# The second layer's modulation: chunk sums on VectorE, ScalarE and GpSimd instead of TensorE matmuls over all chunks

## The reference, cut to what matters

```
m = jax.nn.silu(cond) @ ada_w[layer] + ada_b[layer]      # cond: c or c_ctx, 1024 values; ada_w[layer]: 1024 x 6144
sh1, sc1, g1, sh2, sc2, g2 = m reshaped to 6 x 1024
h = rmsnorm(x, norm_g[layer, 0]) * (1 + sc1) + sh1
x = x + g1 * mixer(h)                                    # layer 0: convolution and retention; layer 1: attention
h = rmsnorm(x, norm_g[layer, 1]) * (1 + sc2) + sh2
x = x + g2 * (square(relu(h @ mlp_w1[layer])) @ mlp_w2[layer])
```

## Time and profile before

| | |
|---|---|
| median of three runs | 1569.05 us (1568.49 to 1569.4) |
| profiled execution, its span from first to last instruction | 1567.7 us; no time of its own is given beside the runs' |
| TensorE busy | 1546.3 us, 99% |
| VectorE, ScalarE, GpSimd busy | 986.4 (63%), 625.8 (40%), 487.8 us (31%) |
| strips of both layers on TensorE (L783) | 43.2 us |
| granted TensorE clock, mean | 0.996 |

### The profile page before, as it was taken

One profiled execution on the slowest core, in us unless ns is written; L12 is line 12 of the kernel. 1 busy time (PEld: TensorE's weight loads), 2 busy tenths in 40 slices (PEclk: granted clock), 3 DMA queues, 4 the chain that ended last, 5 costly groups with the idle time before them and its releaser, 6 DMA issues.

```text
span 1567.7 us, 28790 instructions
## 1 busy us (share of the span) xinstructions
PE 1546.3 (99%) x11992; PEld 1512.9 (97%) x11992; DVE 986.4 (63%) x1831; ACT 625.8 (40%) x1152; POOL 487.8 (31%) x350
## 2 busy tenths in 40 slices
PE   8999999999999999999999999999999999999998
PEld 7999999999999999999999999999999999999998
DVE  5348677675774755565555888773675755556555
ACT  5323333344432344234235534662433334523443
POOL 0233313314222344143235253101333334324431
PEclk9999999999999999999999999999999999999999
DMA  9454333313243344344343121001222132223212
GB/s 327 158 188 142 122 116 114 102 55 110 80 159 111 122 131 138 109 135 148 101 155 134 35 81 61 28 2 54 81 81 59 63 108 68 84 66 108 68 54 82
DMA packets 133410, 162.23 MB, mean 103 GB/s; under 512 B 4640, under 2 KB 108064, under 8 KB 133280
## 3 DMA queue, kind: packets, MB, share of 16 engines
q1 hardware_dynamic: 132048, 159.34, 31.6%
...
## 4 chain that ended last, share of the span: by engine, by line
PE 90%; DVE 5%; ACT 2%; issue 1%; DMA 1%; SPq 0%; POOL 0%; DVEq 0%; ACTq 0%
PE ps L664 59%; PE ps L1083 19%; PE ps L783 3%; PE ps L1275 2%; PE ps L1223 1%; DVE ps L1906 1%; PE ps L920 1%; PE ps L953 1%; DVE hL L1917 1%; DMA pre_w<-in_ada_w 1%; PE ps L869 1%; DVE ps L1896 1%; PE ps L949 1%; DVE amx L2503 1%; ACT wH L1319 1%
## 5 line engine op out<-in xcount | busy, mean ns | idle before, releaser
L1831 POOL TENSOR_TENSOR wL<-raw,wH 128x512 fp32r<-128x512 f32 x212 | 314.7, 1509 | 708.5 <-ACT wH L1319 513.7
L664 PE MATMUL ps<-fH,wH 128*128 128x320 f32 x1024 | 318.8, 311 | 0.2 <-DVE fL L2289 0.2
L664 PE MATMUL ps<-fH,wL 128*128 128x320 f32 x1024 | 316.6, 309 | 0.0
L664 PE MATMUL ps<-fL,wH 128*128 128x320 f32 x1024 | 316.6, 309 | 0.0
L1867 DVE SCALAR_TENSOR_TENSOR xT<-ps,modT,xT 128x192 f32<-128x192 f32 (+1 forms) x456 | 183.3, 434 | 192.0 <-PE ps L664 190.1
L1831 POOL TENSOR_TENSOR wL<-raw_high,wH 128x512 fp32r<-128x512 f32 x124 | 164.2, 1349 | 338.5 <-ACT wH L1342 209.7
L664 PE MATMUL ps<-hH,wH 128*128 128x320 f32 x704 | 221.3, 314 | 1.9 <-DVE hL L1917 1.1
L664 PE MATMUL ps<-hH,wL 128*128 128x320 f32 x704 | 217.8, 309 | 0.0
L664 PE MATMUL ps<-hL,wH 128*128 128x320 f32 x704 | 217.7, 309 | 0.0
L664 PEld LDWEIGHTS ps<-fH,wH 128*128 128x128 f32 x1024 | 192.5, 188 | 3.4 <-DVE xT L1867 1.2
L664 PEld LDWEIGHTS ps<-fL,wH 128*128 128x128 f32 x1024 | 192.5, 188 | 0.1
...
## 6 DMA issues: line engine op xcount, KB each, us to landing
...
raw<-in_mlp_w SPq DMA_DIRECT2D x64, 512.0 KB, 3.8
raw_high<-in_mlp_w SPq DMA_DIRECT2D x64, 512.0 KB, 3.8
raw<-in_even_w_in SPq DMA_DIRECT2D x28, 512.0 KB, 5.9
pre_w<-in_ada_w SPq DMA_DIRECT2D x16, 512.0 KB, 9.1
raw<-in_odd_w_qkv SPq DMA_DIRECT2D x10, 512.0 KB, 3.5
raw<-in_even_w_out SPq DMA_DIRECT2D x8, 512.0 KB, 3.6
raw<-in_odd_w_o SPq DMA_DIRECT2D x6, 512.0 KB, 3.5
```

The costliest lines, as they stand in the source:

```text
L664: last = nc.tensor.matmul(ps[:, bank, 0:width], a_, b_, start=(k == 0 and p_ == 0), stop=(k == nk - 1 and p_ == 2))
L1831: last = nc.gpsimd.tensor_tensor(wL[:, at % 4, cs], raw(t)[:, j, cs], wH[:, at % 4, cs].bitcast(F32), ALU.subtract)
```

## The change

Layer 1's modulation is no longer contracted on TensorE over eight chunks of 128 rows. For each condition s (c and c_ctx) the sum over chunks k of siluc[k, s] x ada[k] is formed elementwise (128 rows x 512 columns), and TensorE only sums its 128 partitions.

- **Loads.** `load_late(i)`, i = 0 to 47, loads 256 rows x 512 columns (512 KB, two chunks) into one half of `ada`, alternately. It waits until GpSimd is done with part i-2.
- **VectorE, `sum0(i)`:** two instructions of 128x512, ada_sum0 = part x siluc + ada_sum0 for c (the first of a block only multiplies).
- **ScalarE, `scale1(i)`:** waits for `sum0(i)`, then scales both chunks in place by c_ctx's values.
- **GpSimd, `sum1(i)`:** waits for that and adds both chunks to ada_sum1 (one instruction for the first part of a block, two for the others).
- **TensorE, `strips_of_sums(b)`:** after four parts, 8 matmuls: stationary a column of ones, moving ada_sum0, then ada_sum1.
- **Places.** Six slots per cycle: `LATE_AT(c, slot)` = 6c - 3 + slot, for parts 0 to 39. Slots 0, 1, 2 lie in the w1 half of a cycle, slots 3, 4, 5 in w2 (VectorE: after updates 5, 8, 14). TensorE's strips stand at slot 0 (after T3), 2 (after w2's first block) and 4 (before w2's last two groups), wherever a block is complete there. Parts 40 to 47 lie in the output projection and the start of layer 1's MLP; strips 10 stand after group 5 of the projection.
- The turned modulation adaT has one buffer instead of two; coefficients(3) and the last modulations move from the end of layer 0's MLP to the projection and to layer 1's first cycle; raw_high moves to the end of SBUF.

The core of the diff:

```diff
+        one_row = vecT[:, 0, R_ROW:R_ROW + 64].rearrange("p (c r) -> p c r", c=2)
...
+        def ada_part(i):
+
+            return ada[:, 2 * (i % 2):2 * (i % 2) + 2, :]
...
+            def load_late(i):
+
+                if i is None:
+                    return
+                if i < 2:
+                    sp.wait_ge(ada_strips, M_MLP)
+                else:
+                    sp.wait_ge(sum1_done, SUM1_AT(i - 1))
+                m, row0 = i // 4, 256 * (i % 4)
+                sp.dma_start(ada_part(i), ada_w[1, row0:row0 + 256, 512 * m:512 * m + 512]
+                             .rearrange("(k p) n -> p k n", p=P)).then_inc(late_in[i % 2], 16)
...
+                w1(0, 1)
+                late(0, 4)
...
                     w2(c, 0, (0, 1))
                     w2(c, 1, (0,))
-                    if layer == 0 and c:
-                        load_ada(M_MLP + 3 * c + 1)
+                    if c:
+                        late(c, 1)
+                        late(c, 2)
                     w2(c, 1, (1,))
-                    if layer == 0 and c == 0:
-                        load_ada(M_MLP + 1)
-                    if layer == 0:
-                        load_ada(M_MLP + 3 * c + 2)
                     if c < CYCLES - 1:
-                        w1(c + 1)
+                        if c:
+                            late(c, 3)
+                        w1(c + 1, 0)
+                        w1(c + 1, 1, (0,))
+                        if c:
+                            late(c, 4)
+                        w1(c + 1, 1, (1,))
+                        late(c, 5)
+                        late(c + 1, 0)
...
+            load_late(LATE - LATE_WO)
+            load_late(LATE - LATE_WO + 1)
             load_tile(T_WO + 3, k8(odd_w_o[0], 768))
+            for i in range(LATE - LATE_WO + 2, LATE):
+                load_late(i)
...
+            def strips_of_sums(b):
+
+                pe.wait_ge(sum0_done, 8 * b + 8)
+                pe.wait_ge(sum1_done, SUM1_AT(4 * b + 4))
+                pe.wait_ge(ada_turn, MOD_LAYER0 + b)
+                pe.wait_ge(vec_in, 16)
+                for c, total in enumerate((ada_sum0, ada_sum1)):
+                    by_lane = total[:].rearrange("p (b j r) -> p j b r", j=4, r=32)
+                    for j in range(4):
+                        last = nc.tensor.matmul(ps[32 * j:32 * j + 32, B_ADA, 0:P], one_row[:, c], by_lane[:, j],
+                                                start=(c == 0), stop=(c == 1), tile_position=(0, 32 * j))
+                last.then_inc(late_strips, 1)
...
-                part(0)
...
                     one(T3, S3, 0, m)
-                part(1)
+                strips_after(c, 0)
...
+                def strips_after(c, slot):
+
+                    i = LATE_AT(c, slot)
+                    if layer == 0 and i is not None and i % 4 == 3:
+                        strips_of_sums(i // 4)
...
-                        if layer == 0:
-                            hooks = {5: [lambda: strips(M_MLP)], 7: [lambda: strips(M_MLP + 1)]}
+                        if layer == 1:
+                            hooks = {5: [lambda: strips_of_sums(11)]}
...
-                        if q == 1:
-                            part(c)(2)
+                            if q == 3 and j == 1:
+                                strips_after(c, 4)
+                        if q == 0:
+                            strips_after(c, 2)
...
-                       (lambda half, k: pe.wait_ge(attn_ready, max(VALUES_OF["tiles", k], VALUES_OF["context", k // GRP]) + 1)) if t == 0 else None)
+                       (lambda half, k: pe.wait_ge(attn_ready, max(VALUES_OF["tiles", k], VALUES_OF["context", k // GRP]) + 1)) if t == 0 else None,
+                       {1: [lambda: strips_of_sums(10)]} if t else None)
...
+            def scale1(i):
+
+                if i is None:
+                    return
+                act.wait_ge(sum0_done, 2 * i + 2)
+                for k in range(2):
+                    last = nc.scalar.activation(ada_part(i)[:, k, :], ada_part(i)[:, k, :], ACT.Copy,
+                                                scale=siluc[:, 2 * (i % 4) + k, 1:2])
+                last.then_inc(scaled1, 1)
...
                         split_product(s, T1, t, g + 2)
+                        late(c, 0)
                         split_product(s, T4, t, g + 4)
                         hidden_pair(c, 0)
                         split_product(s, B22, t, g + 6)
                         split(t + 2, g + 8, (0,))
+                        late(c, 1)
                         hidden_pair(c, 2)
                         split(t + 2, g + 10, (1,))
                         hidden_pair(c, 4)
                         split(t + 3, g + 12, (0,))
+                        late(c, 2)
                         hidden_pair(c, 6)
                         split(t + 3, g + 14, (1,))
...
+                        if q != 2:
+                            late(c, (3, 4, None, 5)[q])
...
+                    if n < 2:
+                        scale1(40 + n)
                     square(3, n, V_WO, "tile")
+                    if n in (4, 5, 7):
+                        scale1({4: 42, 5: 43, 7: 44}[n])
                 split(T_WO + t + 2, G_WO + 4 * (t + 1))
             for n in range(8, 12):
                 square(3, n, V_WO, "tile")
+                if n > 8:
+                    scale1(45 + n - 9)
...
+            def sum1(i):
+
+                if i is None:
+                    return
+                pool.wait_ge(scaled1, i + 1)
+                a, b = (ada_part(i)[:, k, :] for k in range(2))
+                if i % 4 == 0:
+                    if i:
+                        pool.wait_ge(late_strips, i // 4)
+                    nc.gpsimd.tensor_tensor(ada_sum1[:], a, b, ALU.add).then_inc(sum1_done, 1)
+                else:
+                    for k, part in enumerate((a, b)):
+                        pool.wait_ge(sum1_done, SUM1_AT(i) + k)
+                        nc.gpsimd.tensor_tensor(ada_sum1[:], ada_sum1[:], part, ALU.add).then_inc(sum1_done, 1)
...
+            for c in range(1, CYCLES):
+                SUMS_AFTER[T_MLP0 + 4 * c + 2, 0] = (LATE_AT(c, 1),)
+                SUMS_AFTER[T_MLP0 + 4 * c + 3, 0] = (LATE_AT(c, 2),)
+                if c < CYCLES - 1:
+                    SUMS_AFTER["p", c + 1 - PLAIN, B11] = (LATE_AT(c, 3), LATE_AT(c, 4))
+                    SUMS_AFTER["p", c + 1 - PLAIN, B21] = (LATE_AT(c, 5), LATE_AT(c + 1, 0))
...
-                dve.wait_ge(ada_strips, 2 * block + 2)
-                nc.vector.transpose(adaT[:, block % 2, :], ps[:, B_ADA, 0:P]).then_inc(ada_turn, 1)
+                if block < MOD_LAYER0:
+                    dve.wait_ge(ada_strips, 2 * block + 2)
+                else:
+                    dve.wait_ge(late_strips, block - MOD_LAYER0 + 1)
+                if block:
+                    dve.wait_ge(mod_done, block)
+                else:
+                    dve.wait_ge(pre_mod, 4)
+                nc.vector.transpose(adaT[:], ps[:, B_ADA, 0:P]).then_inc(ada_turn, 1)
                 dve.wait_ge(ada_turn, block + 1)
                 m0 = N_PRE + 4 * block
-                nc.vector.tensor_tensor(modT[:, m0:m0 + 4, :], adaT[:, block % 2, :].rearrange("p (b c) -> p b c", c=32)[:, :, 0:2],
+                nc.vector.tensor_tensor(modT[:, m0:m0 + 4, :], adaT[:].rearrange("p (b c) -> p b c", c=32)[:, :, 0:2],
                                         vecT[:, 1, m0:m0 + 4, None].to_broadcast([P, 4, 2]), ALU.add).then_inc(mod_done, 1)
...
+            def sum0(i):
+
+                if i is None:
+                    return
+                dve.wait_ge(late_in[i % 2], 16 * (i // 2 + 1))
+                if i % 4 == 0 and i:
+                    dve.wait_ge(late_strips, i // 4)
+                for k in range(2):
+                    by, part = siluc[:, 2 * (i % 4) + k, 0:1], ada_part(i)[:, k, :]
+                    if i % 4 == 0 and k == 0:
+                        nc.vector.tensor_scalar(ada_sum0[:], part, by, None, ALU.mult).then_inc(sum0_done, 1)
+                    else:
+                        dve.wait_ge(sum0_done, 2 * i + k)
+                        nc.vector.scalar_tensor_tensor(out=ada_sum0[:], in0=part, scalar=by, in1=ada_sum0[:],
+                                                       op0=ALU.mult, op1=ALU.add).then_inc(sum0_done, 1)
...
+                    if n in (1, 2):
+                        sum0(46 + n - 1)
...
+                def late(c, slot):
+
+                    before = 6 * c - 3 + slot
+                    if layer == 0 and 0 < before <= LATE - LATE_WO and before % 4 == 0:
+                        modulation(MOD_LAYER0 + before // 4 - 1)
+                    if layer == 0:
+                        sum0(LATE_AT(c, slot))
...
-                    modulate(c, 0)
+                    late(c, 0)
                     t_lo(s, T4)
                     for m in range(2):
...
-                    modulate(c, 1)
+                    late(c, 1)
...
```

(13 more changed lines are left out.)

85 lines of the change are left out of this document (47 added, 38 removed).

## The result

The changed kernel takes **1625.99 us** (median of 4 runs, 1625.68 to 1626.18), the kernel before 1569.22 (4 runs). The ratio is 1.0362, with a 95% interval from 1.0347 to 1.0377. Slower, as forecast, but by 56.8 us instead of 29, and outside the range.

The account below looks back on a forecast made before the run. TensorE was taken as the bound: 19.6 us saved there, against waits of 30, 8.2, 8.3 and 2.3 us, made +29.2 on a median of 1569.05, so 1598 us, range 1572 to 1613.

Parts of the forecast that it names:

- What bounds: Whole kernel: TensorE, busy 1546.3 of 1567.7 us, is the bound; by sums the other engines have room.
- Saved on TensorE, 19.6 us: Layer 1's modulation: fewer small matmuls and strips at 0.78 us a block take 19.6 us off TensorE.
- Term 1: Start of w2, cycles 2 to 6: new sums and scalings delay it 6.0 us, five times, 30 us.
- The bound without the port, 13: Term 1's lower bound at w2: with no wait for GpSimd, 2.6 us a cycle, 13 in all.
- Term 2: Output projection: eleventh strips wait 5.2 us behind update 5's square, scaling and GpSimd's sum; statistics matmul 3.0 us; 8.2.
- Term 3: Inside w2, cycles 1, 3, 5: strips before the last two groups wait for their own sum, 8.3 us.
- Term 4: Strips behind T3 in cycles 1, 3, 5, 7: 1.4 us in cycle 1, 0.3 in the others, 2.3 us.
- Rival 4: VectorE becomes the bound in w2 and TensorE waits there too: +12 us, 1610; chance 0.09.
- the clock falls as well: TensorE's clock drops behind the waits, 1.5 us more each, up to 9 in all: 1607; chance 0.17.
- "Nothing" for SyncE's loads: SyncE's weight loads, now behind waits for GpSimd's sums, land before they are needed: no cost.

Follow-up runs that it names:

- the last run: Changed kernel with VectorE's running sum in PSUM and sums, scalings and strips re-placed in cycles and output projection, same arithmetic: 1564.87 us, ratio 0.9973 against the kernel before.
- the run with that line moved: Changed kernel with slot 1's two scalings on ScalarE put behind hidden pair 2 instead of ahead of it: 1614.31 us, ratio 1.0286.
- the narrow sums: Changed kernel with GpSimd adding only 64 of 512 columns in all its sums but a block's first: 1609.88 us, ratio 1.0257.
- the fillers: Changed kernel with 36 extra unread matmuls of 320 columns before w2's first one in cycles 2 to 6: 1623.37 us, ratio 1.0339.

## Why the prediction was wrong, step by step

**What bounds.** Right: all of the loss is TensorE's, and the other engines' sums would have fitted.

**Saved on TensorE, 19.6 us.** Right by the rows, but up to 3 us of it do not show in the whole. Strips that start at 669.74 let the second next matmul start at 670.56, 0.82 us later, where it was 1.26; with the 0.24 ahead and without two matmuls' 0.294 that is 0.77 a block, and I had 0.78. But TensorE's busy time less what the low clock adds to it (its work there x 0.45, see below) is 1543.7 before, 1526.8 in the changed kernel and 1527.2 in the last run: 16.8 and 16.5 less. Part of the difference are matmuls that start up again behind waits; the trace was not taken further apart.

**Term 1, 30 us.** Measured 30.6, five waits of 5.58 to 6.94. The total is right, and so is the chain: ScalarE stands 3.96 us in front of slot 1's scaling (the run with that line moved takes back 11.6 us of w2's waits). That GpSimd "must be busy there" was right too: it is the weights' low parts that hold the port, as the narrow sums showed. The bound without the port, 13, was too low: with the sums' stretch gone 19.6 remain.

**Term 2, 8.2 us.** Measured 6.54 + 3.50 = 10.0. The size is near, the reason was wrong: the step named ScalarE's square as what decides ("which no overlap can take away"), and scaling part 43 sooner gained nothing. I counted one sum of 2.65 on GpSimd, and there are two, 5.34 us, behind low parts that end at 1128.15.

**Term 3, 8.3 us.** Measured 3.49, 1.60 and 1.60, where I had 3.5, 2.4 and 2.4. **Term 4, 2.3 us:** 1.34 in cycle 1, and none in cycles 3, 5 and 7.

**Missing from the sum:** cycle 1's w2, where TensorE waits 1.60 for a hidden piece and 2.21 and 0.47 for updates, 4.3 us. Rival 4 had VectorE as the bound in w2 in all cycles; it was so in this one, with the Strassen sums beside the new ones.

**The step that failed is the clock.** I forecast waits of 6 us at 2.4 GHz on both sides, gave "the clock falls as well" 0.17 and priced it at 1.5 us a wait by the one stretch of rows 12. With waits of 48.8 forecast and 55.2 measured the waits explain 6.4 of the missing 27; the other 20.5 are TensorE's busy time over the forecast. TensorE works 45.3 us at the low clock, 39.5 more than before. At 0.267 us a matmul instead of 0.147 these cost 39.5 x (1 - 0.147/0.267), about 18 us. That leaves some 3 us that are not the clock. The last run has as many: 4.5 us over the forecast, of which its 3.3 us more of work at the low clock make 1.5.

The argument that stood against the rival, "work on both sides of the wait is dense", is wrong: the added waits of 3.36 us in the kernel before, with equally dense work, brought the low clock each time, and the fillers took it away. The price was low too: at rows 12 the granted clock was 0.64 and 21 matmuls ran in 4.7 us; behind the 6-us waits of cycles 2 and 6 it is 0.50, with 17 in 4.45 or 4.50. So even the rival as I priced it, 1607, is 19 us short of the measured time. How much of the 18 us would be won if the clock alone were cured stays open: the fillers brought back 6.7 us of matmul time and only 2.6 us of the total.

The Trainium skill (TensorE: Matmul & The Clock Gate, Why this matters for your kernels) had warned of idle gaps between bursts of matmuls. The traces agree on the five waits of 3.36 us and on all of 5.6 us and more, but not on every gap of this kind: see the last section.

**"Nothing" for SyncE's loads.** Right for the weights of the changed kernel (VectorE never waits for them; it waits once for a part, the last one, 4.3 us, a landing that term 2 had counted), but a thin margin: as soon as slots moved, weights came late by up to 4.8 us.
